# Sliding attention layer in woven steps, and the bias row store ahead of the first projection

## Chip, cores and metric

One Trainium2 chip, one core. The metric is the device time of one execution in microseconds, the lower the better. The kernel runs TensorE (matmuls; its weight loads are shown as PEld), VectorE (DVE), ScalarE (ACT), GpSimd (POOL) and the DMA engines; SyncE (SP) issues the weight DMAs, ScalarE's queue the others.

## What is computed

Two blocks in a row on 512 tokens of 1024 features, float32. The first block has two layers (a mixer, a convolutional feed-forward and a gated embedding each); the second block has one layer of two attentions and an expert layer. The change touches the second layer's mixer:

```python
def mixer_c(h, w_in, q_norm, k_norm, sinks, rel_bias, w_out):
    proj = h @ w_in
    q, k, v = jnp.split(proj, [SW_HEADS * SW_DIM, (SW_HEADS + SW_KV_HEADS) * SW_DIM], axis=-1)
    q = rmsnorm(q.reshape(B, S, SW_HEADS, SW_DIM), q_norm)
    k = rmsnorm(k.reshape(B, S, SW_KV_HEADS, SW_DIM), k_norm)
    ...
        logits = jnp.einsum('bqhgd,bkhd->bhgqk', qn, kn) * scale + bias
        logits = jnp.where(mn, logits, -jnp.inf)
        m = jnp.maximum(jnp.max(logits, axis=-1, keepdims=True), sink)
        e = jnp.exp(logits - m)
        w = e / (jnp.sum(e, axis=-1, keepdims=True) + jnp.exp(sink - m))
        return jnp.einsum('bhgqk,bkhd->bqhgd', w, vn)
    ...
    return o.reshape(B, S, C_OUT) @ w_out
```

There are 16 query heads and 4 key heads of 64 features; blocks of 128 queries see their own block of keys and the one before (the first block only its own). The bias is a table of distances (`window_rows`); a similar table (`chunk_rows`) serves the second block. Both tables are built at the start, from the inputs.

## The kernel before

Activations are kept by feature: a tile is 128 features by 512 tokens. Every weight product is made in three matmuls of 128x512 a k-step, from operands split into a high and a low part (`split_product`, L189). Weights come as one stream of slots of 16 tiles (1 MB). SyncE loads a slot into `weights_raw`; GpSimd splits it (L2608 makes the high part, L2610 the low part) into one of two places in `weights_split`; TensorE frees a place with the first matmul of the next slot (`release_previous`). So GpSimd splits a slot each time TensorE enters a new one.

`program` lists the stages; each engine runs its part of each stage in this order, and where a stage has `meet=True` all three engines wait for each other at its end. Layers other than the two touched here mostly do without meetings: they hand PSUM banks on one by one (`Bank`, `Held`), in an order that the program writes out.

`mixer_ab` (first layer's mixer): inputs are loaded by ScalarE's queue, `first_norm` norms them, `normed_heads` projects 20 tiles and the values (L189; VectorE evacuates at L1195, ScalarE the values at L594), and then the stage of `bias_rows` makes the bias rows: TensorE multiplies a small table (L1462), VectorE makes the chunk rows (L1468, L1470) and copies the window rows (L1473), ScalarE issues two DMAs that store them 128 times over (L1477, L1480). A meeting ends it. The stick-breaking attention (L879, L909) follows. In `normed_heads` the first tile goes ahead of the norm's sums; every evacuation needs `rstd`, which waits for ScalarE's square root (L481) and VectorE's reciprocal (L492). There are eight banks.

`mixer_c` (the sliding attention layer) has these stages, with a meeting after each but the last: `normed_heads` for 8 query and 2 key tiles and the values (L1509, L594); a norm stage for these ten tiles (squares L1547, sums L1521, root L1554, reciprocal L1530, product L1533) and eight copies of keys (L1560); `softmax_attention` in a loop of four rounds of 16 units (a head and a query block each: score L1266, bias L1319, maximum L1325, shift L1330, exponent L1420 and that of the sink L1423, transpose L1280, copy L1430, values L1290, scaling by the inverse L1377); `turn_split` (L822) back to features; `residual_product`, whose tiles are added to the residual (L621) and normed for the feed-forward (L444, L453, L460).

`branches` (the second block's attentions) is unchanged. It has steps of two scores (L1747), with dense k-steps between them (L189), the turn of the step before (L1764), and the value products of the step before that (L1785); on VectorE biased scores (L1886), small sums (L1893, L1895), joining (L1898); on ScalarE exponents (L2015).

## Time and profile before

| | us |
|---|---|
| median of 3 runs (lowest, highest) | 3805.36 (3803.27, 3808.34) |
| profiled execution, its own time | 3805.51 |
| its span from first to last instruction | 3803.7 |
| TensorE busy | 3556.4 (93%) |
| VectorE busy | 2068.8 (54%) |
| ScalarE busy | 922.9 (24%) |
| GpSimd busy | 1829.8 (48%) |

Shares are over the whole span; TensorE's ends are modelled, so 93% does not mean that it works at its peak. The chain that ended last is TensorE for 80% of the span and L189 alone for 71%. Mean granted clock of TensorE is 0.949 of full speed; of the 40 slices of the page it is 0.8, 0.8, 0.5, 0.5 in those from 856 to 1236 us.

### The profile page before, as it was taken

What the parts mean: (1) busy time and instruction counts of PE and PEld (TensorE: products, weight loads), DVE (VectorE), ACT (ScalarE), POOL (GpSimd) and SP (SyncE); (2) the same over time, 40 slices, a digit from 0 to 9 for tenths busy, and PEclk for the clock granted to TensorE, in tenths of its full rate; (3) what the DMA queues carried; (4) which work ended last, traced back from release to release, by engine and by line L of the source; (5) the groups of instructions that cost most, each with busy time, mean ns of one, the idle gap of its engine ahead of it and who ended that gap; (6) DMA issues with size and microseconds to landing.
All of it is one profiled execution on the core that took longest, in us unless ns stands there. A gap on an engine that the chain in (4) does not pass through costs nothing.

```text
span 3803.7 us, 44488 instructions
## 1 busy us (share of the span) xinstructions
PE 3556.4 (93%) x16442; PEld 2914.4 (77%) x16442; DVE 2068.8 (54%) x3513; ACT 922.9 (24%) x1682; POOL 1829.8 (48%) x548
## 2 busy tenths in 40 slices
PE   7865699998789999989999999999999999999999
PEld 6754588887556788878677878888888888888887
DVE  2125564426454645161662288885555437777776
ACT  1054322202144222020453121113333311111111
POOL 5500156654300556555333556665444456666664
PEclk9987799998855999999999999999999999999999
DMA  3250032222200222222111223434444475655552
GB/s 140 93 56 0 11 105 90 99 100 78 78 0 11 95 97 92 100 94 89 56 62 67 100 93 140 143 140 161 179 193 182 172 249 197 201 180 204 192 188 100
DMA packets 134077, 439.85 MB, mean 116 GB/s; under 512 B 7019, under 2 KB 76692, under 8 KB 97044
## 3 DMA queue, kind: packets, MB, share of 16 engines
q1 hardware_dynamic: 39168, 285.23, 21.3%
q10 hardware_dynamic: 94740, 152.22, 12.1%
q8 instruction: 124, 2.03, 0.2%
q14 instruction: 45, 0.37, 0.0%
HBM read 362.46 MB, written 74.96 MB: 115 GB/s over the span
## 4 chain that ended last, share of the span: by engine, by line
PE 80%; DVE 5%; ACT 2%; issue 1%; ACTq 0%; DVEq 0%; DMA 0%
PE banks L189 71%; PE banks L2218 3%; PE banks L1266 1%; DVE memory L460 1%; PE banks L1290 1%; DVE memory L1898 1%; DVE memory L1530 1%; PE banks L1280 1%; PE banks L1785 1%; ACT memory L2015 1%; PE banks L1747 1%; DVE memory L453 0%; PE banks L1764 0%; DVE memory L1895 0%; PE banks L468 0%
## 5 line engine op out<-in xcount | busy, mean ns | idle before, releaser
L189 PE MATMUL banks<-memory,weights_split 128*128 128x512 f32 x9456 | 2217.9, 394 | 57.9 <-DVE memory L453 31.5
L189 PEld LDWEIGHTS banks<-memory,weights_split 128*128 128x128 f32 x9456 | 1772.2, 189 | 448.7 <-DVE memory L453 35.2
L2608 POOL TENSOR_SCALAR weights_split<-weights_raw 128x2048 fp32r<-128x2048 f32 x272 | 543.5, 1998 | 1927.1 <-issue 1130.5
L2610 POOL TENSOR_TENSOR weights_split<-weights_raw,weights_split 128x2048 fp32r<-128x2048 f32 x272 | 1286.1, 4728 | 22.7
L189 PE MATMUL banks<-weights_split,memory 128*128 128x512 f32 (+1 forms) x3648 | 817.4, 386 | 0.0
L189 PEld LDWEIGHTS banks<-weights_split,memory 128*128 128x128 f32 x3648 | 678.3, 188 | 138.4
L2366 DVE TENSOR_TENSOR memory<-memory,memory 128x512 f32<-128x512 f32 x128 | 356.0, 2782 | 51.1 <-DMA memory<-hidden 44.5
L2351 DVE TENSOR_SCALAR memory<-banks,memory 128x128 f32<-128x128 f32 x512 | 174.4, 403 | 210.4 <-PE banks L2218 204.8
L2372 DVE TENSOR_TENSOR memory<-memory,memory 128x512 fp32r<-128x512 f32 x128 | 176.6, 1379 | 160.9 <-ACT memory L2486 160.9
L2486 ACT ACTIVATE memory<-memory 128x512 fp32r<-128x512 f32 x128 | 80.7, 632 | 601.1 <-PE banks L189 579.2
L2419 ACT ACTIVATE memory<-banks 128x512 f32<-128x512 f32 x128 | 76.5, 597 | 550.7 <-PE banks L189 550.7
L666 DVE TENSOR_TENSOR banks<-banks,memory 128x512 f32<-128x512 f32 x88 | 61.3, 699 | 231.8 <-PE banks L189 231.8
L621 DVE TENSOR_TENSOR residual<-banks,residual 128x512 f32<-128x512 f32 x32 | 22.1, 690 | 222.6 <-PE banks L189 222.6
L2431 ACT ACTIVATE memory<-banks 128x512 f32<-128x512 f32 x128 | 131.6, 1133 | 21.0 <-PE banks L2218 21.0
L714 ACT ACTIVATE memory<-banks,memory 128x512 f32<-128x512 f32 x88 | 68.6, 781 | 263.3 <-DVE banks L666 263.3
L2218 PEld LDWEIGHTS banks<-memory,memory 128*128 128x128 f32 x1024 | 124.1, 191 | 5.0
L2218 PE MATMUL banks<-memory,memory 128*128 128x128 f32 x1024 | 124.5, 275 | 0.0
L460 DVE TENSOR_TENSOR memory<-memory,memory 128x512 f32<-128x512 f32 x56 | 123.9, 2212 | 0.0
L444 ACT ACTIVATE memory<-residual,memory 128x512 fp32r<-128x512 f32 x64 | 46.2, 722 | 320.0 <-DVE residual L621 273.6
L453 DVE SCALAR_TENSOR_TENSOR memory<-residual,memory,memory 128x512 fp32r<-128x512 f32 x64 | 96.3, 1504 | 33.3 <-ACT memory L444 33.3
L1124 PE MATMUL banks<-memory,memory 128*128 128x128 f32 x256 | 47.5, 351 | 49.0 <-DVE memory L1049 47.4
L1266 PE MATMUL banks<-memory,memory 64*128 64x256 f32 (+1 forms) x128 | 66.8, 643 | 26.1 <-DVE memory L1579 26.1
(237 smaller groups left out, 2510.8 us busy)
## 6 DMA issues: line engine op xcount, KB each, us to landing
weights_raw<-in_weights SPq DMA_DIRECT2D x272, 1024.0 KB, 4.8
hidden<-memory ACTq DMA_DIRECT2D x64, 512.0 KB, 2.6
routing<-memory ACTq DMA_DIRECT2D x16, 2048.0 KB, 6.3
memory<-routing ACTq DMA_DIRECT2D x32, 1024.0 KB, 6.5
memory<-hidden ACTq DMA_DIRECT2D x32, 1024.0 KB, 8.9
window_rows<-memory ACTq DMA_DIRECT2D x1, 3064.0 KB
chunk_rows<-memory ACTq DMA_DIRECT2D x1, 2556.0 KB
residual<-in_x ACTq DMA_DIRECT2D x4, 512.0 KB, 11.3
```

The source lines that it names most:

```text
L189: last = k.nc.tensor.matmul(out, left[a], right[b], start=start and n == 0, stop=stop and n == 2, skip_group_check=True)
L453: v.scalar_tensor_tensor(out=self.out.low(n), in0=cut(k.h, n * 512, 512), scalar=k.column(self.gain, n), in1=self.out.high(n).bitcast(F32) ...
L460: v.tensor_tensor(self.total, self.squares[0] if n == 1 else self.total, self.squares[n % 2], ALU.add).then_inc(k.summed, 1)
L1266: k.nc.tensor.matmul(k.banks[:, u % 3, 0:blocks * P], query, key, start=True, stop=True).then_inc(scored, 1)
L2218: last = mm(score_banks[g % DEPTH].memory[:, s], rows[g % DEPTH][:, s], cols[g % DEPTH][:, s], start=True, stop=True, skip_group_check=True)
L2351: last = v.tensor_scalar(rows[g % DEPTH][:, t * P:(t + 1) * P], iota, cut(turned, at, 1), cut(turned, 2 * TOKENS + at, 1), ALU.is_equal, A ...
L2366: v.tensor_tensor(gated[e % 2].rearrange("p (c t) -> p c t", c=TOKENS // PORTION), cut(kept[place], e % GROUP * 512, 512).rearrange("p (c ...
L2372: v.tensor_tensor(operand.low(e % 4), gated[e % 2], operand.high(e % 4).bitcast(F32), ALU.subtract).then_inc(ready, 1)
L2431: a.activation(by_token[:, at:at + BATCH, :], score_banks[g % DEPTH].memory.rearrange("p (t n) -> p t n", t=BATCH), ACT.Copy).then_inc(mat ...
L2486: a.activation(operand.high(e % 4), gated[e % 2], ACT.Copy).then_inc(high_made, 1)
L2608: k.nc.gpsimd.tensor_scalar(high, raw, 1.0, 1.0, ALU.mult, ALU.mult).then_inc(k.high_made, 1)
L2610: k.nc.gpsimd.tensor_tensor(low, raw, high.bitcast(F32), ALU.subtract).then_inc(k.weights_ready[place], 1)
```

## The change

The kernel after has a function `window_layer` in place of `mixer_c` and `softmax_attention`. It works on pairs of heads (PAIRS = 8), four steps a pair, 32 steps. Ahead of the steps come four product tiles (two of keys, first two of queries), their norms and the values. Each step issues the scores of a pair for one query block, a k-step of a later weight product, the turn of the probabilities of the step before, sometimes the square sums of a later query tile, another k-step, and the value products of two steps before. The k-steps are those of the other six query tiles and then of the output product. The turn is a matmul with a diagonal matrix that holds the inverse of the totals, so that it transposes and divides at once; the value product gives its result by feature. Scores carry the opposite sign, and bias, smallest value and sink are taken in one VectorE instruction. The weight tiles are reordered to fit. In `mixer_ab` the stage of the bias rows goes ahead of the projection, has no meeting, and stores the window rows negated; the projection now ends with a meeting.

```diff
@@ -1197,9 +1197,10 @@
...
-    projected = normed_heads(k, first, 20, evacuate, 2, 512, lambda part, b: cut(values, b * 1024 + part * 512, 512))
     load_rows, rows_stage, await_rows = bias_rows(k)
-    stages = [Stage(scalar=load_all, meet=False), normed_first, projected, rows_stage]
+    projected = normed_heads(k, first, 20, evacuate, 2, 512, lambda part, b: cut(values, b * 1024 + part * 512, 512),
+                             meet=True)
+    stages = [Stage(scalar=load_all, meet=False), normed_first, rows_stage, projected]
     with k.scope(at=HN_AT):
...
-        v.tensor_copy(rows[0:SW_HEADS, :], bank.memory[0:SW_HEADS, 0:BUCKET_ROWS]).then_inc(k.freed["vector"], 1)
+        v.tensor_scalar(rows[0:SW_HEADS, :], bank.memory[0:SW_HEADS, 0:BUCKET_ROWS], -1.0, None,
+                        ALU.mult).then_inc(k.freed["vector"], 1)
...
-    return load, Stage(tensor, vector, scalar), await_written
+    return load, Stage(tensor, vector, scalar, meet=False), await_written
...
+    score_banks = [Held(k, 2 + f, (biased, 2 * STEPS - 1 + f)) for f in range(2)]
+    turn_banks = [Held(k, 4 + f, [free for w, free in enumerate(turn_free) if w % 2 == f][-1]) for f in range(2)]
+    out_banks = [Held(k, 6 + f, (k.x_low, mixed.made_before + PAIRS - 1 + f)) for f in range(2)]
...
+        def score(t):
+            i, n = t // 4, t % 4
+            if t == 0:
+                pe.wait_ge(keys_made, 2 * SW_KV // 2)
+                pe.wait_ge(keys_copied, SW_KV)
+            if n == 0:
+                pe.wait_ge(q_made, i + 1)
+            for f in range(2):
+                if t == 0:
+                    score_banks[f].await_free(pe)
+                else:
+                    pe.wait_ge(biased, 2 * (t - 1) + f + 1)
+                rows = slice(64 * f, 64 * f + 64)
+                mm(cut(score_banks[f].memory, 0, width(t)), normed_q[i % 2][rows, n * P:(n + 1) * P],
+                   cut(key_pairs[rows, :], i // 2 * 512 + (n + 1) * P - width(t), width(t)), start=True,
+                   stop=True).then_inc(scored, 1)
...
+        def turn_probs(t):
+            bank = await_turn_bank(turn_uses["probs", t])
+            pe.wait_ge(turning_made, 2 * t + 2)
+            for f in range(2):
+                for at in range(0, width(t), P):
+                    last = mm(cut(bank, f * 256 + at, P), cut(buffer(t, f), at, P), turn_matrix(t, f), start=True,
+                              stop=True)
+            last.then_inc(turned_up, 1)
...
+            pe.wait_ge(copied, t + 1)
+            bank = out_banks[i % 2].memory
+            for at in range(0, width(t), P):
+                block = n + 1 - (width(t) - at) // P
+                for f in range(2):
+                    last = mm(bank[64 * f:64 * f + 64, n * P:(n + 1) * P],
+                              cut(values, block * 256 + i // 2 * 64, 64), cut(turned[t % 3], f * 256 + at, P),
+                              start=at == 0, stop=at + P == width(t), skip_group_check=True)
...
+            for tiles, parts in (((0, 1, 2, 3), range(6)), ((0, 1, 2, 3), (6,)), ((0, 1, 2, 3), (7,)),
+                                 ((4, 5, 6, 7), range(8))):
...
+        opening_product(0)
+        normed.tensor_sums(pe)
+        opening_product(1)
+        opening_product(2)
+        opening_sums(0)
+        opening_sums(1)
+        opening_product(3)
+        opening_sums(2)
+        opening_values(0)
+        opening_sums(3)
+        for b in range(1, BLOCKS):
+            opening_values(b)
...
+        for t in range(STEPS + 2):
+            late = t >= STEPS
+            if t < STEPS:
+                score(t)
+            advance(2 if late else 1)
+            if 1 <= t <= STEPS:
+                turn_probs(t - 1)
+            if ("sums", (t + 3) // 4) in turn_uses and t % 4 == 1:
+                sum_squares((t + 3) // 4)
+            advance(4 if late else 1 if t < 24 or t % 4 in (0, 1, 3) and t != 29 and t != 31 else 0)
+            if t >= 2:
+                apply(t - 2)
+        for _ in work:
+            pass
...
+            v.tensor_tensor_reduce(out=buffer(t, f), in0=cut(score_banks[f].memory, 0, width(t)),
+                                   in1=cut(table, at, width(t)), scale=1.0,
+                                   scalar=cut(minus_sinks, 2 * i + f, 1), op0=ALU.add, op1=ALU.min,
+                                   accum_out=one(shift, t, f)).then_inc(biased, 1)
...
+        def shift_sinks(t):
+            dve.wait_ge(biased, 2 * t + 2)
+            v.tensor_tensor(pair(sink_shift, t), pair(shift, t), cut(minus_sinks, t // 4 * 2, 2),
+                            ALU.subtract).then_inc(sinks_shifted, 1)
+
+        def turn_matrices(t):
+            dve.wait_ge(sinks_exped, t + 1)
+            v.tensor_tensor(pair(total, t), pair(total, t), pair(sink_exp, t), ALU.add).then_inc(small_made, 1)
+            dve.wait_ge(small_made, 2 * t + 2)
+            v.reciprocal(pair(inverse, t), pair(total, t)).then_inc(small_made, 1)
+            dve.wait_ge(small_made, 2 * t + 3)
+            for f in range(2):
+                v.tensor_scalar(turn_matrix(t, f), k.const("ident"), one(inverse, t, f), None,
+                                ALU.mult).then_inc(turning_made, 1)
+
+        def invert_half(i, half):
+            dve.wait_ge(rooted, i - 1)
+            part = cut(deviation, half * 256, 256)
+            v.reciprocal(part, part).then_inc(inverted, 1)
+
+        def normalise(i):
+            dve.wait_ge(inverted, 4 + 2 * (i - 1))
+            v.scalar_tensor_tensor(out=normed_q[i % 2], in0=raw_q, scalar=k.column("q_norm"), in1=deviation,
+                                   op0=ALU.mult, op1=ALU.mult).then_inc(q_made, 1)
...
+        for n in range(4):
+            evacuate(made[n], first_raw[n], 1.0 if n < 2 else -(64 ** -0.5))
+        opening_keys(0)
+        opening_keys(1)
+        opening_queries(0)
+        opening_queries(1)
+        for t in range(LAST + 1):
+            i = t // 4
+            if t < STEPS:
+                for f in range(2):
+                    biased_scores(t, f)
+                shift_sinks(t)
+            if t % 4 == 0 and 2 <= i + 1 < PAIRS:
+                evacuate(dense[i - 1], raw_q, -(64 ** -0.5))
+            if t >= 6 and t % 4 == 2:
+                low(i - 1)
+            if t < STEPS:
+                turn_matrices(t)
+            if 2 <= i + 1 < PAIRS:
+                if t % 4 >= 2:
+                    invert_half(i + 1, t % 4 - 2)
+                if t % 4 == 3:
+                    normalise(i + 1)
+        for n in range(D_TILES + 1):
...
+        def exponent(t, f):
+            act.wait_ge(biased, 2 * t + f + 1)
+            a.activation(buffer(t, f), buffer(t, f), ACT.Exp, bias=one(shift, t, f), scale=-1.0,
+                         accum_out=one(total, t, f)).then_inc(exped, 1)
+
+        def sink_exponents(t):
+            act.wait_ge(sinks_shifted, t + 1)
+            act.wait_ge(exped, 2 * t + 2)
+            a.activation(pair(sink_exp, t), pair(sink_shift, t), ACT.Exp).then_inc(sinks_exped, 1)
...
+        for t in range(LAST + 1):
+            i = t // 4
+            if t >= 6 and t % 4 == 2:
+                high(i - 1)
+            if t < STEPS:
+                for f in range(2):
+                    exponent(t, f)
+                sink_exponents(t)
+            if 1 <= t <= STEPS:
+                copy(t - 1)
+            if t % 4 == 0 and 2 <= i + 1 < PAIRS:
+                square(i + 1)
+            if t % 4 == 1 and 2 <= i + 1 < PAIRS:
+                root(i + 1)
...
-            lambda: mixer_c(k, common, mix1_norm, ffn_norm[1]), lambda: layer(1),
+            lambda: window_layer(k, common, mix1_norm, ffn_norm[1]), lambda: layer(1),
...
-    tiles += [feature(c[:, 0:1280], 8), by_token(c[:, 1280:1536]), feature(a["c_w_out"][0], 8)] + layer_rest(1)
+    window_out = feature(a["c_w_out"][0], 8).reshape(8, 8, P, P)
+    tiles += [feature(c[:, 1024:1280], 8), feature(c[:, 0:256], 8), by_token(c[:, 1280:1536]), feature(c[:, 256:1024], 8)]
+    tiles += [window_out[:4, 0:6].reshape(-1, P, P), window_out[:4, 6], window_out[:4, 7], window_out[4:].reshape(-1, P, P)]
+    tiles += layer_rest(1)
```

## Rows read from the trace of the kernel before

**Rows 1.** Busy us by stretch: PE, PEld, DVE, ACT, POOL; clock, DMA share, GB/s.
```profile
180.00:200.00 20.00, 0.64 (x2) 0.00 (x0) 0.65 (x2) 0.83 (x2) 0.00 (x0) 0.63 0.47 58
...
936.60:1005.00 68.40, 67.71 (x325) 57.13 (x325) 10.82 (x13) 3.79 (x7) 32.62 (x10) 0.93 0.24 81
...
1005.00:1055.40 50.40, 15.68 (x20) 4.07 (x20) 41.26 (x22) 17.07 (x28) 0.00 (x0) 0.59 0.13 42
...
1055.40:1215.10 159.70, 143.60 (x464) 101.09 (x464) 84.73 (x390) 69.16 (x260) 0.00 (x0) 0.50 0.00 0
...
1860.00:1960.00 100.00, 95.78 (x498) 71.08 (x496) 80.09 (x181) 53.38 (x130) 34.29 (x11) 1.00 0.15 53
```

**Rows 2.** Timeline of the sliding attention layer: start us, us, engine, line, operation.
```profile
936.57 1.65 PE L189 MATMUL banks<-memory,weights_split 128*128 128x512 f32 x3 [5.98 <-DVE memory L453]
...
949.32 0.69 DVE L1509 TENSOR_TENSOR memory<-banks,memory 128x512 f32<-128x512 f32 x1 [4.56 <-PE banks L189]
...
992.64 11.67 PE L189 MATMUL banks<-weights_split,memory 128*128 128x256 f32 x96
...
1266.64 0.69 DVE L621 TENSOR_TENSOR residual<-banks,residual 128x512 f32<-128x512 f32 x1 [1.10 <-PE banks L189]
...
1275.15 9.03 PE L189 MATMUL banks<-memory,weights_split 128*128 128x512 f32 x27 [3.79 <-DVE memory L453]
```

**Rows 3.** Timeline of TensorE in the steps of `branches`.
```profile
1853.62 0.64 PEld L1785 LDWEIGHTS banks<-memory,memory 128*128 128x128 f32 x4
...
1854.38 0.30 PEld L1747 LDWEIGHTS banks<-memory,memory 64*128 64x128 f32 x4
...
1854.80 1.23 PEld L189 LDWEIGHTS banks<-memory,weights_split 128*128 128x128 f32 x6
...
1859.32 0.70 PE L1747 MATMUL banks<-memory,memory 64*128 64x256 f32 x4
...
1859.95 1.24 PEld L189 LDWEIGHTS banks<-memory,weights_split 128*128 128x128 f32 x6 [0.33 <-issue]
...
1863.65 1.09 PEld L1785 LDWEIGHTS banks<-memory,memory 128*128 128x128 f32 x8
...
1864.86 0.30 PEld L1747 LDWEIGHTS banks<-memory,memory 64*128 64x128 f32 x4
```

**Rows 4.** Timeline, VectorE and ScalarE operations that overlap no split by GpSimd.
```profile
317.46 0.48 DVE L984 TENSOR_SCALAR memory<-memory,memory 128x512 f32<-128x512 f32 x1
...
1020.23 3.35 DVE L1530 RECIPROCAL memory<-memory 128x512 f32<-128x512 f32 x1
...
1853.77 0.75 DVE L1898 SCALAR_TENSOR_TENSOR memory<-memory,memory,memory 128x512 f32<-128x512 f32 x1
...
1862.78 0.41 DVE L1886 CUSTOM_DVE_ANT_0 memory<-banks,memory 128x256 f32<-128x256 f32 x1
...
1863.23 0.51 ACT L2015 ACTIVATE memory<-memory,memory 128x256 f32<-128x256 f32 x1 [5.12 <-DVE memory L1886]
...
1864.36 0.16 DVE L1893 RECIPROCAL memory<-memory 128x1 f32<-128x1 f32 x1 [0.81 <-ACT memory L2015]
```

**Rows 5.** Timeline, VectorE beside GpSimd's second operation of a split.
```profile
138.85 4.70 DVE L1470 TENSOR_SCALAR memory<-memory 8x256 f32<-8x256 f32 x1
...
1857.44 4.76 DVE L1898 SCALAR_TENSOR_TENSOR memory<-memory,memory,memory 128x128 f32<-128x128 f32 x1
1857.49 4.56 POOL L2610 TENSOR_TENSOR weights_split<-weights_raw,weights_split 128x2048 fp32r<-128x2048 f32 x1
```

**Rows 6.** Timeline of the first layer's start and of the bias rows.
```profile
29.10 0.68 DVE L460 TENSOR_TENSOR memory<-memory,memory 128x512 f32<-128x512 f32 x1
...
60.26 0.69 DVE L1195 SCALAR_TENSOR_TENSOR memory<-banks,memory 128x512 f32<-128x512 f32 x1 [4.75 <-PE banks L189]
...
181.26 17.87 ACTq L1480 DMA_DIRECT2D window_rows<-memory  x1
...
199.90 0.43 DVE L909 COPY memory<-memory 128x512 f32 x1 [18.67 <-ACTq L2576]
```

515 lines of the change are left out of this document (239 added, 276 removed).

## Prediction

> **What bounds the kernel now.** I read the windows first. In the fourth layer part, the sliding attention, TensorE works at its upper clock level while the dense products run, then stands almost idle for 50.4 us (15.7 busy), then spends 159.7 us in the attention at a granted clock of 0.50, the lower of the two levels (1.2 GHz), with VectorE at 84.7 us, ScalarE at 69.2 and GpSimd, which splits the weights, at nothing; TensorE's 143.6 are stretched by the clock and by ends that are only modelled [rows 1]. So this stretch is bound less by one engine than by a chain that passes from one to the next, and the weight stream stands still meanwhile. The last window of [rows 1] is the other attention of this kernel, `branches`, which already puts dense products between its steps: clock 1.00, TensorE 95.8 of 100 us busy. It is the best model of the new layer, and most of my prices come from it. Second, the timeline of the layer's landmarks: it begins with three products at 936.57, and the feed-forward after it can go on at 1275.15 [rows 2]. That is 338.6 us, of which the dense work is small: a tile of eight k-steps takes 0.69 + 4.75 = 5.44 us [rows 6], so a k-step ("partial", three matmuls) takes 0.68 us, and a value block 11.67 / 4 = 2.9 us [rows 2]. 10 and 8 tiles and 4 value blocks are 98 + 12 = 110 us. Third, the timeline around 180 us for the bias rows: the last ACT issue takes 17.87 us, and the next stage waits for it [rows 6].
>
> **Part one, the opening.** Removed: the norm stage and the three meetings around it. New: TensorE makes two key tiles, two query tiles, four square sums and the values, and VectorE norms only these four tiles. TensorE: the second tile is ready at 949.3 as before, then two tiles to 954.8 and about 961.7 with two sums of 0.75 us between, then sum, value, sum and three values: 974.9. (A square sum is one f32 product of 512 columns in two passes: 2 x 0.227 from the tile time, and 0.2 to 0.4 of fill as at the changes in [rows 3].) VectorE is later. From 962.6 it has four reciprocals of 3.35 us [rows 4] and six operations from SBUF of 0.75 [rows 4]. GpSimd's second operation of a split locks such operations out for its whole length: an operation on 128 columns shows 4.76 us, where the same on 512 columns takes 0.75 when GpSimd rests [rows 4], and a tensor_scalar of eight rows shows 4.70 [rows 5]. Splits start with each slot of 16 partials (962.9, about 980.5 here) and last 6.6 us (32.6 for ten instructions [rows 1]; the second 4.6 [rows 5], so the first about 2). So: reciprocal to 966.0, key writes held until 969.5 and done at 970.9; second keys 975.7; first queries 979.8. The first score then goes at 980.0, 5.1 us after TensorE ran dry. Its first partial starts the next split, the second queries' reciprocal ends at 983.3, and its last write is held until 987.9. Only then come the biased scores of step 0, and step 1 starts at 988.7. TensorE is cold there (lower level, as in every gap of [rows 1]); with this, steps 1 to 3 take 5, 4.5 and 4.4 us (no value products at first): step 4 starts at 1002.4.
>
> **Part two, one group of four steps.** Prices on TensorE, from start to start of the weight loads [rows 3]: scores of a pair of heads, 0.42 with one key block and 0.63 with two; products of 128x128 f32, 0.76 for four instructions, 1.21 for eight. A step with two key blocks has eight in the turn and eight in the value products, its first step of a group four. The value products have a form that the trace does not show, 64 stationary columns: between 0.6 (two heads side by side) and 1.2 us; I take 1.2, the row nearest to it. Per step score + partial + turn of the step before + partial + values of two steps before: 4.18, 4.70 (with a square sum), 3.95, 4.39 = 17.2 us.
>
> VectorE per step: it begins 0.75 after the score's start [rows 3], a biased score takes 0.41, the pair 0.8, and ScalarE's two exponents begin 0.45 after the first and last 1.1 to 1.2 [rows 4], the sinks' exponent 0.3. Then total, reciprocal and two tiny matrices: the 128x128 tensor_scalar is not in the trace, between 0.15 and 0.55 (its 512-column form [rows 4]); I take 0.2, since a quarter of the columns is nearer to the low end. The turn may start 2.9 us after VectorE began (2.5 with one block). In the third step half a reciprocal (1.7) follows, in the fourth 1.7 + 0.75 for the normed queries of the next pair. Evacuating a query tile and making the low part lie in the wait for the exponents and cost nothing; without that wait they would cost 1.4 us a group.
>
> With a group's first score at 0, scores start at 0, 4.2, 8.9, 12.8; VectorE begins the third step at 9.6 and leaves it at 14.2, begins the fourth only then and has the next queries at 19.8. The next group starts at **19.9**, not 17.2: the waits move from ScalarE's chain to the query norm. At steps 8, 16 and 24 a split begins as well. The turn matrices of that step, due at 3.1, wait for the split's end at 7.25 and are ready at 8.1; the next starts are 11.5 and 15.5, the group takes **22.6**. Groups 1, 3, 5 take 19.9, groups 2, 4, 6 take 22.6, the last one, without norms and with fewer partials, 14.4: 1002.4 + 59.7 + 67.8 + 14.4 = 1144.3.
>
> **Part three, the tail.** Steps 32 and 33 hold twelve partials and the last turn and values, 11.8 us; 112 - 72 = 40 partials remain, 27.2 us; the last product's residual row at 1266.64 to 1275.15 [rows 2] becomes the same 8.7 us with the same lock. The next layer goes on at 1144.3 + 11.8 + 27.2 + 8.7 = 1192.0. **Gain 83.2 us.** The reordered weight tiles are as many as before and cost nothing: GpSimd needs 6.6 us for a slot that TensorE never eats in under 10.9. Table loads of ScalarE's square root fall into its idle time.
>
> **Part four, bias rows.** The row product, two rows on VectorE and two DMA issues go ahead of the projection. Behind it, only the meeting remains: VectorE's 199.90 becomes about 181.3 (ScalarE had done its value copies when it came to the issue at 181.26), **18.6 us** [rows 6]. In front, TensorE's 0.8 us falls into waits that it has anyway. ScalarE however has the 17.87 us issue before the square root on which all banks' release waits: VectorE's norm is done at 29.8, the rows and the first issue at 32, the second until 50, root and reciprocal until 56, first bank free at 57. TensorE has five further free banks and needs the sixth at 60.2, where [rows 6] has the fifth one emptied. Slack 3 us. If weights (DMA share 0.24 in the dense stretch [rows 1]) stretch the issue by as much, it is 2 us late. Between 0 and 5 us of loss I take 1: 17.6 us gain.
>
> **Sum.** The profiled execution took 3805.5 us (span 3803.7 and 1.8 around it), 0.1 over the median. 3805.5 - 83.2 - 17.6 = 3704.7, say **3704**.
>
> **Rivals.**
> A, *shorter groups*. If the value products of the two heads run side by side (0.6), a plain group takes 18.8 and a locked one 22.0, the other stretches 5 less: 3693. With VectorE's chain alone as bound (2.5 + 2.95 + 4.65 + 5.6 and links, 16.5 a group) it would be 3684. The Trainium skill, "TensorE: Matmul & The Clock Gate", section on packing small matmuls, says that matmuls with outputs in distinct column groups run concurrently; that is this rival, and no row of the trace before shows the form. Chance 0.16.
> B, *locks twice*. The split may catch the matrices of step 8j and again the queries' write or the tiny subtraction for the sinks, since it starts when TensorE reaches the slot, not at a fixed place. One more lock of 4.6 us in each of four slots: 3722. Chance 0.15.
> C, *the row stage gains nothing*: the issue takes long under the weight loads and the projection stops for all of it. For it: the DMA share is 0.47 behind the old place with almost no weights moving [rows 1]. Against it: five free banks. 3722. Chance 0.08.
> D, *the turn is dear*. Before, the turn was a transpose against the identity; now it is a true f32 product. If its passes were twice as dear as the value products of `branches` (0.22 us more for each of 14 blocks a group, 3.1 us, of which 1.3 reach the end of a plain group), the layer is 9 to 12 us longer: 3714. The Trainium skill, the same page, table of terms, has a transpose mode that is 4 times faster for FP32, which speaks against this fold; [rows 3] show 1.21 us for eight true f32 instructions. Chance 0.04.
> E, *the clock stays at its lower level*. The old attention had 0.50, the gap before step 1 is there, and each locked group has a wait of 2.6 us. In the steps alone that would give about +85: 3790, chance 0.03. The slower side: it stays from the first wait through the tail. 112 partials cost 0.68 more each (76), and the small products, 94 us at the upper level, 70 more, less some 32 of waits that they fill: +115, **3820**. It decides from 102 us of loss on. Against it: `branches` has waits of the same kind at 1.00 [rows 1]. Chance 0.02.
> F, the change does not take effect in the order written (nothing moves): 3805, chance 0.01.
>
> **How the numbers follow.** The forecast has 0.51. Its own doubt is about 10 us. The range must hold the forecast, A to D, so from A's lower end to B and C with that doubt: 3674 to 3738. Measurement tells 0.2% (7.6 us) from no change; faster by more: all but E's second case, F and part of E's first, 0.95; within: 0.02; slower: 0.03.
>
> **What would show it.** Window 980 to 1145 at clock about 1.00 with TensorE over 85% busy; first score near 980 and a gap behind it; starts of the scores of steps 8, 12, 16, 20 19 to 23 us apart, with the longer ones where a split begins; VectorE's tensor_scalar of a locked step at 4 us or more; ScalarE's square root of the first norm near 51 to 56 us; VectorE's first copy of the stick-breaking stage near 181. If groups take under 17 or over 25 us, or the clock falls below 0.9 in the steps, the sum is wrong.

## The result, and the profile after

The kernel after takes 3720.24 us (median of 4 runs, 3718.21 to 3722.16), the kernel before beside it 3804.51 (3803.27 to 3808.34): ratio 0.978, 95% interval 0.976 to 0.979. The forecast was 3704 with a range from 3674 to 3738. The direction, the size and the layer that pays were right; the gain came out 84 us, not 101. The profiled execution took 3722.16, its span is 3720.3 (before 3803.7), mean granted clock 0.970 (before 0.949). TensorE's busy time fell from 3556.4 to 3494.7 us only: the rest of the gain is idle time that is gone.

Page of the kernel after, parts 1 and 2: busy time, and the granted clock in 40 slices of 93 us.
```profile
span 3720.3 us, 43665 instructions
...
PE 3494.7 (94%) x16522; PEld 2867.9 (77%) x16522; DVE 2058.2 (55%) x3418; ACT 921.5 (25%) x1623; POOL 1829.0 (49%) x548
...
PEclk9987799999889999999999999999999999999999
```
The two slices at 0.5 are gone; those of the new layer stand at 0.8 and 0.8.

Timeline of the kernel after, the same landmarks as [rows 2, 6].
```profile
191.78 0.43 DVE L909 COPY memory<-memory 128x512 f32 x1 [43.89 <-ACTq L2689]
...
930.76 1.65 PE L189 MATMUL banks<-memory,weights_split 128*128 128x512 f32 x3 [5.97 <-DVE memory L453]
...
1151.34 32.30 PE L189 MATMUL banks<-memory,weights_split 128*128 128x512 f32 x141
...
1187.42 8.95 PE L189 MATMUL banks<-memory,weights_split 128*128 128x512 f32 x27 [3.79 <-DVE memory L453]
```
The difference of the spans, 83.4 us, taken apart by them:

| stretch | before | after | gain | predicted |
|---|---|---|---|---|
| to VectorE's first copy of stick-breaking (L909) | 199.90 | 191.78 | 8.1 | 17.6 |
| stick-breaking, L909 to L970 | 111.4 | 113.8 | -2.5 | 0 |
| from there to the sliding layer | 625.3 | 625.1 | 0.2 | 0 |
| sliding layer | 338.58 | 256.66 | 81.9 | 83.2 |
| everything behind it | 2528.6 | 2532.9 | -4.3 | 0 |

So the sliding layer met its forecast within 1.3 us, and the shortfall of 17 us lies in the bias rows (9.5), in stick-breaking and behind the layer.

Windows of the kernel after in the new layer: the opening, then groups of four steps (cut at the first score of each); the last row is the last group with the two late steps. Columns as in [rows 1].
```profile
930.76:974.60 43.84, 38.59 (x189) 31.61 (x190) 24.37 (x17) 12.46 (x20) 13.03 (x4) 0.89 0.25 89
974.60:994.70 20.10, 15.54 (x74) 10.43 (x74) 14.91 (x38) 6.21 (x23) 6.74 (x2) 0.75 0.24 83
994.70:1014.00 19.30, 15.06 (x102) 10.26 (x100) 12.31 (x41) 11.07 (x29) 0.00 (x0) 0.95 0.01 2
1014.00:1037.50 23.50, 17.54 (x100) 11.97 (x100) 17.41 (x41) 11.07 (x29) 6.44 (x2) 0.86 0.13 45
1037.50:1059.20 21.70, 17.45 (x98) 12.06 (x99) 12.29 (x41) 11.07 (x29) 0.00 (x0) 0.88 0.00 1
...
1127.10:1151.30 24.20, 24.17 (x147) 18.32 (x147) 7.62 (x37) 7.89 (x26) 6.20 (x2) 0.93 0.00 1
```
A group with a split on GpSimd (6.44 us in the POOL column) takes 23.2 to 23.5 us, one without 21.5 and 21.7, the first without 19.3. TensorE is busy for 15.1 to 17.5 us of a group, at a granted clock of 0.86 to 0.95. What it waits for, by the view of waits for 974 to 1151 us, TensorE (us in total, times, longest):
```profile
PE banks L1422 <- DVE memory L1590: 25.5, 6, 4.3
PE banks L1438 <- DVE memory L1580: 10.0, 7, 3.5
PE banks L1422 <- DVE memory L1547: 5.3, 1, 5.3
```
The first line is the score of a new pair behind VectorE's product of the next queries, at the end of every group with a norm. The second is the turn behind its diagonal matrices. The timeline shows both, at the end of a group and in the locked step behind it:
```profile
1011.39 1.74 DVE L1586 RECIPROCAL memory<-memory 128x256 f32<-128x256 f32 x1
1013.17 0.75 DVE L1590 SCALAR_TENSOR_TENSOR memory<-memory,memory,memory 128x512 f32<-128x512 f32 x1
...
1013.98 0.80 PE L1422 MATMUL banks<-memory,memory 64*128 64x128 f32 x4 [4.24 <-DVE memory L1590]
...
1014.70 1.65 PE L189 MATMUL banks<-memory,weights_split 128*128 128x512 f32 x3
...
1017.66 4.54 POOL L2723 TENSOR_TENSOR weights_split<-weights_raw,weights_split 128x2048 fp32r<-128x2048 f32 x1
...
1017.82 4.67 DVE L1580 TENSOR_SCALAR memory<-memory,memory 128x128 f32<-128x128 f32 x2
...
1020.32 0.97 PE L189 MATMUL banks<-memory,weights_split 128*128 128x512 f32 x3
...
1022.64 0.68 PE L1438 MATMUL banks<-memory,memory 128*128 128x128 f32 x4 [1.35 <-DVE memory L1580]
```
Two things are to be seen. The second half of the reciprocal and the product stand behind everything else of the fourth step. And the same three matmuls take 1.65 us right behind the wait and 0.97 six us later: the granted clock falls to its lower level with the gap, so a wait is paid for twice.

The opening of the kernel after, weights of the first projection (for POOL, what its idle time ended with):
```profile
30.80 18.45 ACTq L1269 DMA_DIRECT2D window_rows<-memory  x1
...
50.57 0.69 ACT L481 ACTIVATE memory<-banks,memory 128x512 f32<-128x512 f32 x1
...
66.67 1.91 POOL L2721 TENSOR_SCALAR weights_split<-weights_raw 128x2048 fp32r<-128x2048 f32 x1 [10.12 <-DMA weights_raw<-in_weights]
...
73.38 23.62 PE L189 MATMUL banks<-memory,weights_split 128*128 128x512 f32 x96 [2.09 <-POOL weights_split L2723]
99.61 23.66 PE L189 MATMUL banks<-memory,weights_split 128*128 128x512 f32 x96 [2.61 <-POOL weights_split L2723]
125.12 22.05 PE L189 MATMUL banks<-memory,weights_split 128*128 128x512 f32 x96 [1.85 <-POOL weights_split L2723]
147.00 43.68 PE L189 MATMUL banks<-weights_split,memory 128*128 128x512 f32 x192
```
Three times GpSimd waits 10 to 12 us for a slot that has not landed, and TensorE about 2 us behind it. Behind the first two of these waits TensorE falls to the lower clock (0.67 and 0.66 in the 5 us that follow; 23.6 us for 96 matmuls where the last line has 43.68 / 2 = 21.8). Behind the third it does not (1.00, and 22.05 us). In the kernel before, the value products that start here at 147.00 start at 136.22.

### The profile page after: what moved, and what is told of

Same layout as the page of the kernel before. It is cut to its first block, busy times and chain, and to the rows that moved or that the text cites. A ratio compares the mean times of both kernels' runs of the same rounds, so it can differ in the third digit from the quotient of the medians.

```text
span 3720.3 us, 43665 instructions
## 1 busy us (share of the span) xinstructions
PE 3494.7 (94%) x16522; PEld 2867.9 (77%) x16522; DVE 2058.2 (55%) x3418; ACT 921.5 (25%) x1623; POOL 1829.0 (49%) x548
## 3 DMA queue, kind: packets, MB, share of 16 engines
q1 hardware_dynamic: 39168, 285.23, 21.5%
## 4 chain that ended last, share of the span: by engine, by line
PE 78%; DVE 6%; ACT 3%; issue 1%; DMA 0%; ACTq 0%; DVEq 0%
PE banks L189 71%; PE banks L2331 3%; DVE memory L460 1%; DVE memory L2011 1%; PE banks L1898 1%; ACT memory L2128 1%; PE banks L1860 1%; DVE memory L1586 1%; ACT memory L1662 1%; PE banks L1438 0%; DVE memory L453 0%; DVE memory L1532 0%; PE banks L1877 0%; DVE memory L2008 0%; PE banks L468 0%
## 5 line engine op out<-in xcount | busy, mean ns | idle before, releaser
L189 PE MATMUL banks<-memory,weights_split 128*128 128x512 f32 x9456 | 2249.8, 396 | 44.2 <-DVE memory L453 30.8
L2467 DVE TENSOR_TENSOR memory<-banks,memory 128x512 f32<-128x512 f32 x128 | 87.2, 681 | 0.0
```

The costliest lines, as they stand in the source:

```text
L189: last = k.nc.tensor.matmul(out, left[a], right[b], start=start and n == 0, stop=stop and n == 2, skip_group_check=True)
L2467: v.tensor_tensor(cols[g % DEPTH].rearrange("p (t n) -> p t n", t=BATCH), iota.unsqueeze(1).broadcast_to(three), cut(turned, TOKENS + g * ...
```

## Experiments

**The bias rows: where did 9.5 us go?** Theory 1: the two stores (2556 and 3064 KB by the page's list of DMA issues) share the DMA engines with the weights, and the weights come late. Rival: the move brings what was predicted, and the shortfall is elsewhere. Two kernels move this stage alone, one in each direction.

```diff
-    stages = [Stage(scalar=load_all, meet=False), normed_first, rows_stage, projected]
+    stages = [Stage(scalar=load_all, meet=False), normed_first, projected, rows_stage]
```


> The kernel after with the bias rows stage put back behind the first projection (and the meeting of the engines put back). Theory 1, late weights: in the kernel after the two stores of bias rows share the DMA engines with the projection's weights, so the move gains only the 8.1 us by which VectorE's first copy of the stick stage comes earlier (191.78 against 199.90); this run is 3720.2 + 8 = about 3728 us. Rival, the prediction's own term: the move is worth 17.6 us and the shortfall is elsewhere; this run is 3720.2 + 17.6 = about 3738 us.

Measured: 3724.6 us (ratio to before 0.979, interval 0.978 to 0.980). So the change of the sliding layer alone is worth 80.2 us beside its kernel before (3804.8).

The same edit the other way round, in the kernel before (with the meeting moved along):

> The kernel before with the bias rows stage moved ahead of the first projection, and nothing else. Theory 1, late weights: 3804.5 - 8 = about 3796 us. Rival, the prediction's own term: 3804.5 - 17.6 = about 3787 us. If the two parts of the change help or hinder each other, this run and the one that undoes the move will not show the same difference.

Measured: 3798.9 us (ratio 0.998, interval 0.997 to 0.999). The two runs give 4.4 and 5.9 us for the move: even less than theory 1 said, and far from 17.6. The executions of the second spread widely, from 3791 to 3807 us, and the profiled one is the longest of them. In it TensorE waits 9.6 us in three waits for late weights, one of 5.1 us:
```profile
73.41 22.05 PE L189 MATMUL banks<-memory,weights_split 128*128 128x512 f32 x96 [2.14 <-POOL weights_split L2611]
100.56 23.58 PE L189 MATMUL banks<-memory,weights_split 128*128 128x512 f32 x96 [5.11 <-POOL weights_split L2611]
126.52 23.62 PE L189 MATMUL banks<-memory,weights_split 128*128 128x512 f32 x96 [2.38 <-POOL weights_split L2611]
```
The run with the old order has none of these waits and starts its value products at 135.09. The list of DMA issues from 28 to 130 us has the weight loads with their median time to landing, first in the kernel after, then in the kernel before:
```profile
weights_raw<-in_weights SPq DMA_DIRECT2D x8, 1024.0 KB, 16.1
```
```profile
weights_raw<-in_weights SPq DMA_DIRECT2D x8, 1024.0 KB, 4.8
```

Now the cause by itself: the larger store is issued behind the projection, all else stays.
```diff
         act.dma_start(k.dram["chunk_rows"], chunk_rows[0:CH_HEADS, :].unsqueeze(1).broadcast_to(
             [CH_HEADS, P, TOKENS + P - 1])).then_inc(written, 16)
+    def store_window(act):
         bank.await_read(act)
         act.dma_start(k.dram["window_rows"], rows[0:SW_HEADS, :].unsqueeze(1).broadcast_to(
             [SW_HEADS, P, BUCKET_ROWS])).then_inc(written, 16)
...
+    def values_then_store(act):
+        evacuate_values(act)
+        store_window(act)
```


> The kernel after, with the larger store (window_rows, 17.9 us of issue on ScalarE) issued behind ScalarE's part of the first projection, not ahead of it. Theory 1, late weights: the weights arrive on time, the projection ends up to 10 us earlier, and ScalarE issues the store while the next stage's first loads are awaited; 3720.2 - 10 = about 3710 us, or down to nothing gained if ScalarE's issue now holds up the stick stage's first steps. Rival, the store is not what makes the weights late (other loads do): 3720 us.

Measured: 3709.9 us (ratio 0.975, interval 0.973 to 0.976), 10.4 us under the kernel after. Timeline of this run:
```profile
30.30 0.82 ACTq L1273 DMA_DIRECT2D chunk_rows<-memory  x1
...
72.12 67.44 PE L189 MATMUL banks<-memory,weights_split 128*128 128x512 f32 x288 [2.08 <-POOL weights_split L2731]
139.40 43.68 PE L189 MATMUL banks<-weights_split,memory 128*128 128x512 f32 x192
...
183.12 0.63 ACTq L1277 DMA_DIRECT2D window_rows<-memory  x1
...
184.52 0.43 DVE L909 COPY memory<-memory 128x512 f32 x1 [44.23 <-ACTq L2697]
```
One of TensorE's three waits is left; GpSimd still waits for two late slots (10.1 and 9.6 us). Not all of the 10.4 us belongs to the edit: of the 9.9 us between the two profiles 7.3 stand at VectorE's first copy (184.52 against 191.78), and 2.8 behind the sliding layer, where the program is the same. And the issue that takes 17.87 us in the kernel before [rows 6], 18.45 in the kernel after and 20.53 in the run before this one takes 0.63 here, with the same bytes: it was long wherever it stood right behind the other store. The rival of the prediction that blames ScalarE's issue (C) falls too: in the kernel after the issue is over at 49.3 and the root runs at 50.57, and TensorE has no wait for a bank in the whole projection. That the stores' traffic makes the weights late, and not their issue, is inferred: with the large store gone from this place the other's issue takes 0.82 us, and slots are late all the same. A kernel that stores 8 of the 128 copies at the old place, which would have parted the two, gave no time.

**The groups: what sets 21.7 us?** Theory 2: VectorE's own order. It begins the fourth step only after its work of the third, and the next queries come at the end of the fourth. First, take the twelve half reciprocals away:
```diff
-                if t % 4 >= 2:
-                    invert_half(i + 1, t % 4 - 2)
...
         def normalise(i):
-            dve.wait_ge(inverted, 4 + 2 * (i - 1))
+            dve.wait_ge(rooted, i - 1)
```


> The kernel after without the twelve half reciprocals of the query norm in the window steps; the queries of head pairs 2 to 7 are multiplied by their root instead of its inverse, so the scores of those pairs differ from the reference. Theory 2, VectorE's own order ends each group: a group of four steps is as long as VectorE's work in it, TensorE waits 4.25 us for the product at its end six times, and without 2 x 1.75 us the wait shrinks to about 0.8: 3720.2 - 6 x 3.5 = about 3699 us. Rival, the prediction's own working (TensorE's instructions and the lock set the group, VectorE's reciprocals are beside them): about 3720 us.

Measured: 3693.3 us (ratio 0.971, interval 0.969 to 0.972), 27 us less, not 21; from the first score to the end of the layer it is 24.0 us (188.8 against 212.8). The wait on L1590 falls from 25.5 us to 4.6 in all. TensorE's instructions and the lock alone do not set the group.

Then the same work, only earlier:
```diff
-            if t < STEPS:
-                turn_matrices(t)
             if 2 <= i + 1 < PAIRS:
                 if t % 4 >= 2:
                     invert_half(i + 1, t % 4 - 2)
                 if t % 4 == 3:
                     normalise(i + 1)
+            if t < STEPS:
+                turn_matrices(t)
```


> The kernel after with VectorE's half reciprocals and the query product issued ahead of the turn matrices of their step, not behind; nothing is left out. Theory 2, VectorE's order ends the group: the first half then lies in the 2.0 us in which VectorE waits for ScalarE's sink exponents (L1575 behind L1668), and the product is ready about 1.7 us earlier in its own step, so the 4.25 us wait of TensorE shrinks to about 1: 3720.2 - 6 x 3.3 = about 3700 us, less what TensorE or the later turn matrices give back. Rival (as for the run without reciprocals): 3720 us, or slower, since the turn matrices come 2.5 us later and the turn waits for them.

Measured: 3693.3 us (ratio 0.971, interval 0.969 to 0.972): the same time without leaving anything out, since the reciprocals now lie where VectorE waited for ScalarE (27.6 us in 32 waits on the sinks' exponent in the kernel after, 11.2 in 17 here). Windows of this run, by group:
```profile
990.01:1006.04 16.03, 15.09 (x101) 10.28 (x99) 11.59 (x38) 11.08 (x29) 0.00 (x0) 1.00 0.01 2
1006.04:1027.08 21.04, 16.67 (x99) 11.09 (x99) 17.37 (x42) 11.10 (x29) 6.43 (x2) 0.92 0.16 51
1027.08:1043.09 16.01, 15.07 (x98) 10.28 (x98) 12.14 (x42) 11.08 (x29) 0.00 (x0) 1.00 0.00 1
```
A group without a split takes 16.0 us, 15.1 of them TensorE's, at clock 1.00. It was 21.7: 3.3 us of wait are gone, as expected, and some 2 us more, because TensorE no longer falls to the lower clock behind the wait. From the first score to the end of the layer the edit is worth 212.8 - 190.3 = 22.5 us, nearly as much as leaving the reciprocals out. So of what both runs gained beyond their forecasts about 3 us (24.0 against 21, 22.5 against 20) come from the steps, and about as much is not their doing: the opening of this run took 40.6 us, not 43.8, by the clock alone, and that of the run before it 40.7. Windows of the first 10 us of the layer, first the kernel after, then this run:
```profile
930.76:935.76 5.00, 5.00 (x14) 3.68 (x15) 1.43 (x2) 1.77 (x3) 0.00 (x0) 0.50 0.46 170
935.76:940.76 5.00, 5.00 (x13) 3.88 (x13) 3.37 (x4) 0.79 (x2) 0.00 (x0) 0.54 0.00 0
```
```profile
929.37:934.37 5.00, 5.00 (x18) 3.66 (x19) 1.63 (x2) 1.93 (x3) 0.00 (x0) 0.72 0.49 179
934.37:939.37 5.00, 5.00 (x23) 4.13 (x22) 3.62 (x5) 0.63 (x1) 0.00 (x0) 1.00 0.00 0
```
The instructions are the same, both follow a wait of 6.0 us, and one has 27 matmuls in its first 10 us, the other 41.

**Does it matter that the products are spread over the steps?** All eight k-steps of a group go into its first step.
```diff
-            advance(2 if late else 1)
+            advance(2 if late else 1 if t >= 24 else 8 if t % 4 == 0 else 0)
...
-            advance(4 if late else 1 if t < 24
+            advance(4 if late else 0 if t < 24 else 1 if t < 24
```


> The kernel after with the 8 partial products of a dense projection placed together in the first step of each of the first six groups, and none in the other three steps; nothing is left out. Theory 2, VectorE's and ScalarE's loop sets the steps: it still takes some 4 us a step without them, the bunch of 7.6 us fills the first step, and the group stays at 21 to 23 us: 3720 us, within 8. Rival, the products are what hides the waits inside each step (the reason for placing them one by one): steps 1 to 3 become as long as before but without 1.9 us of useful work each, which the first step then pays: 6 x 3 x 1.9 = 34 us more, 3754 us.

Measured: 3731.7 us (ratio 0.981, interval 0.980 to 0.983), 11.5 us more than the kernel after: between the two theories, nearer to the first, but outside the 8 us that it allowed. From the first score to the end the layer is 13.6 us longer (226.4 against 212.8). TensorE now waits 24.6 us in 15 waits for the turn matrices (10.0 in 7 before), so the k-steps do cover that wait; the wait for the next queries stays (22.4 us in six). The fine spread is worth 12 to 14 us of the 82; the rest comes from doing the products beside the steps at all, or from other parts of the rewrite, which no run here takes apart.

**Both edits.**

> The kernel after with both edits: the larger store of bias rows issued behind the first projection (measured alone: 3709.9, 10.4 us less) and the query norm ahead of the turn matrices. If the two lie in different layers and do not touch, the gains add: by theory 2, 3720.2 - 10.4 - 20 = about 3690 us; by its rival 3710 us.

Measured: 3688.9 us (ratio 0.969, interval 0.968 to 0.970). It is faster than with either edit alone, but the late store adds 4.4 us here, not 10.4. In the profile VectorE's first copy comes 5.7 us earlier than without it (184.79 against 190.44), and the opening of the layer gives 3.3 back: 43.9 us at clock 0.50 and 0.54, as in the kernel after.

**The lock.** In the run with the early norm a group with a split takes 5.2 us more than one without. Its timeline:
```profile
1007.14 1.90 POOL L2721 TENSOR_SCALAR weights_split<-weights_raw 128x2048 fp32r<-128x2048 f32 x1 [28.55 <-issue]
...
1007.34 1.71 DVE L1570 TENSOR_TENSOR memory<-memory 128x2 f32<-128x2 f32 x1
...
1009.13 4.53 POOL L2723 TENSOR_TENSOR weights_split<-weights_raw,weights_split 128x2048 fp32r<-128x2048 f32 x1
...
1009.58 4.10 DVE L1575 TENSOR_TENSOR memory<-memory 128x2 f32<-128x2 f32 x1
...
1014.54 1.19 PE L1438 MATMUL banks<-memory,memory 128*128 128x128 f32 x4 [3.42 <-DVE memory L1580]
```
Two numbers a partition, 1.71 and 4.10 us. Theory 3: only such operations of VectorE (two inputs, or a tensor_scalar, all in SBUF) are held, so they should leave VectorE in these steps.
```diff
+    def on_scalar(t):
+        return t % 8 < 2
...
+                    a.activation(one(sink_exp, t, f), one(shift, t, f), ACT.Exp,
+                                 bias=k.column("sinks", t // 4 * 2 + f)).then_inc(exped, 1)
...
+                    a.activation(one(total, t, f), one(total, t, f), ACT.Identity,
+                                 bias=one(sink_exp, t, f)).then_inc(sinks_exped, 1)
...
+                a.activation(turn_matrix(t, f), k.const("ident"), ACT.Copy,
+                             scale=one(inverse, t, f)).then_inc(turning_made, 1)
```


> The kernel with both edits (3688.9 us) in which, in the steps 0, 1, 8, 9, 16, 17, 24 and 25, the two sums of the sinks and totals and the two turn matrices are made on ScalarE, and VectorE does only the reciprocal between them; nothing is left out. In the kernel with the early query norm a group with a weight split on GpSimd lasts 21.0 to 21.3 us and one without 16.0, and the 5.2 us between them stand on VectorE's tiny sums of 128x2 (1.71 and 4.10 us, where they take 0.16 elsewhere) beside GpSimd's L2721 and L2723. Theory 3, the lock: those instructions are the ones that wait for GpSimd; on ScalarE they do not, and three groups lose 3 to 4.5 us each and the first some 3: 3688.9 - 12 to 16 = about 3675 us. Rival, GpSimd holds up whatever VectorE does beside it (the reciprocal, the biased scores), or the work on ScalarE lengthens the steps as much: 3689 us, within 3.

Measured: 3676.3 us (ratio 0.966, interval 0.965 to 0.968), 12.6 us less. The locked groups take 17.4 to 18.0 us (21.1 and 21.3 before), the first four steps 18.8 (20.0 before), a gain of 1.2 there and not 3. Timeline:
```profile
1000.92 4.56 POOL L2765 TENSOR_TENSOR weights_split<-weights_raw,weights_split 128x2048 fp32r<-128x2048 f32 x1
...
1002.05 0.48 DVE L1583 CUSTOM_DVE_ANT_0 memory<-banks,memory,memory 128x256 f32<-128x256 f32 x1 [1.02 <-PE banks L1442]
...
1004.82 0.17 DVE L1598 RECIPROCAL memory<-memory 128x2 f32<-128x2 f32 x1 [1.88 <-ACT memory L1698]
```
Beside the same GpSimd operation the biased score (one input in PSUM) and the reciprocal keep their usual 0.48 and 0.17 us. The lock theory holds, and its rival falls. The Trainium skill, "SBUF — State Buffer", section on the two separate sides, has a port pair that the two engines take for a whole instruction, VectorE only in a two-port mode or with two inputs from SBUF; the trace agrees. With only the first of the two steps (`t % 8 == 0`):

> As the run before it, but only in the steps 0, 8, 16 and 24. Theory 3: GpSimd is still in its 4.5 us when the next step's 128x2 sum comes, which is then held for the rest of it, some 2 to 3 us; so about half of the gain is left, 3681 us. Rival: 3689 us, as with both steps.

Measured: 3676.0 us (ratio 0.966, interval 0.965 to 0.967). The lock moves to the next step as expected, 2.54 us of it:
```profile
1004.93 4.58 POOL L2765 TENSOR_TENSOR weights_split<-weights_raw,weights_split 128x2048 fp32r<-128x2048 f32 x1
...
1006.98 2.54 DVE L1592 TENSOR_TENSOR memory<-memory 128x2 f32<-128x2 f32 x1
```
but it costs less than it shows: first score to end of layer is 180.4 us, against 178.2 with both steps and 190.4 with neither. Four fifths of the gain, not half, and in the medians no difference at all. I had counted the lock's length as the loss; it seems that some of it lies under k-steps that TensorE has anyway. The work on ScalarE has a price too: with both steps there, VectorE's reciprocal in the second waits 1.88 us for ScalarE (the line at 1004.82). Which of the two it is, no run takes apart.

## Why the prediction was right, and where it was not

**What bounds the kernel** held: a chain between engines at the lower clock, with the weight stream at rest; the model `branches` [rows 1, 3, 4] gave usable prices.

**Part one.** The first score was put 43.4 us behind the layer's start, with TensorE dry for 5.1; measured 43.9 and 5.3. Step 4 was put at 65.8, measured 63.9. Right, though part of the size is luck: 3 us of it hang on the clock. And the lock fell elsewhere: the last write of queries, put as held for 4.6 us, took 1.19 us (at 977.66), and the tiny subtraction for the sinks behind it 3.82 (at 979.43).

**Part two.** The mechanism was the one named, "the waits move from ScalarE's chain to the query norm", and six waits of 4.25 us show it. The sizes: plain groups 19.3, 21.7 and 21.5 where 19.9 stood, locked ones 23.5, 23.2 and 23.3 where 22.6 stood, 5.0 us more in all. Two terms were mis-sized. The clock: I priced every instruction at the upper level; a score shows 0.49 us there and three matmuls of a k-step 0.97, and behind each wait they show 0.80 and 1.65; `branches` with its mean of 1.00 [rows 1] had misled me. And ScalarE's table loads, said to fall into idle time: behind the root the exponents' load of 1.28 us comes first, and VectorE waits 1.98 us for the sinks' exponent at 1029.80, in the third step, where the group before has 1.60 in its third and 0.85 is usual in others. The price of the value products was wrong the other way: eight take 0.66 us, rival A's price, not 1.2. The Trainium skill, "TensorE: Matmul & The Clock Gate", section on packing small matmuls, has outputs in distinct column groups run at the same time; the trace agrees. It did not matter in the kernel after, where TensorE was not the bound, so rival A's time of 3693 failed while its price was true. It matters once VectorE's order is mended: the run with the early norm reaches 16.0 us a group, below even the 16.5 that rival A gave VectorE's chain, and takes 3693.3.

Rival B, a second lock, is there in the record but not in its price: the 128x2 sums are held as well as the matrices (L1575 1.18 us ahead of L1580's 4.67). A lock cost 1.8 us a group in the kernel after and 5.2 in the faster one: the shorter the chain, the less covers it. The prediction's own signs spoke against it here. It said that the sum is wrong if the clock falls below 0.9 in the steps, and expected about 1.00 with TensorE over 85% busy from 980 to 1145 us; the trace has 0.89 and 78% (129.5 of 165 us). The sum for the layer came out all the same, because the slower groups were made up for elsewhere. And the measured 3720 lies at the 3722 that rivals B and C gave, without either having happened as priced: no bank held up the projection, and the layer took 1.3 us more than put, not 18. D: eight instructions of the turn take 1.05 us busy, about what was put; the Trainium skill's transpose mode (same page, table of terms) was not tried. E: the steps have 0.75 to 0.95, not 0.5; F falls.

**Part three.** The last group and the two late steps took 24.2 us where 14.4 + 11.8 = 26.2 stood, the end 36.1 where 35.9 stood. The lock behind the last product fell where it was put: from the last residual row to the next layer it is 8.5 us (1178.91 to 1187.42), as before (1266.64 to 1275.15), with VectorE held beside GpSimd's split:
```profile
1178.91 0.69 DVE L1628 TENSOR_TENSOR residual<-banks,residual 128x512 f32<-128x512 f32 x1 [1.01 <-PE banks L189]
...
1181.68 5.03 DVE L460 TENSOR_TENSOR memory<-memory,memory 128x512 f32<-128x512 f32 x1
```
So the sum for the layer was out by 1.3 us only because errors of 2 to 5 us stand on both sides: the opening and the last group with the late steps 2 us less each, the six groups 5 us more.

**Part four** was the failure. The step is "If weights (DMA share 0.24 in the dense stretch) stretch the issue by as much, it is 2 us late": it asked what the weights do to the stores' issue and never what the stores do to the weights. The row that said so was there: a DMA share of 0.47 in the stretch behind the old place with almost no weights moving [rows 1]. The Trainium skill, "DMA: Bandwidth & Descriptors", section on issuing engines that are not separate DMA queues, says that transfers of all of them run on the same 16 DMA engines and interleave; the late slots agree with it. Theory 1 is right in kind (late slots, and 10.4 us back without the larger store, 7.3 of them in this stage). Its size, 8.1 us, was read from one profile; by the same mark the runs with the stage moved alone give 7.0 and 5.1 us, and 4.4 and 5.9 in the medians, with 6.5 us of waits in one profile and 9.6 in another.

**What the sum had no term for**: stick-breaking 2.5 us longer, and 4.3 behind the layer. Neither belongs to the change. Stick-breaking, the same program in all kernels, takes 111.4 us in the profile of before and between 109.5 and 114.3 in the others; the 114.3 is of the kernel with the old order of the bias rows. Everything behind the sliding layer takes 2528.6 us in one profile of before and 2532.6 in the profile with only the bias rows moved, which is the same program there; all profiles lie at 2528.6 to 2530.2 or at 2532.6 to 2533.3. What picks the one or the other is open.

## What to carry to other kernels

When a chain runs over several engines, look at the order within one engine first: work for the next round belongs in front of the wait for another engine, not behind it, which was worth nearly as much here as leaving the work out (22.5 against 24.0 us). Price a wait of TensorE with the slower matmuls behind it: most waits of 2 to 5 us here cost some 2 us on top, though two of about 2 us cost only 0.2. Before a store is moved beside a weight stream, count its bytes against that stream, and not only the time of its issue.

## What the runs showed of the hardware

A DMA issue on ScalarE's queue of 3064 KB took 17.9, 18.5 and 20.5 us right behind one of 2556 KB, and 0.63 us when 150 us lay between them. Weight loads of 1024 KB beside these two stores took 16.1 us to landing in the median, 4.8 without them. GpSimd's two operations of a weight split hold VectorE's tensor_scalar and two-input operations from SBUF for as long as they last, down to two columns (0.16 us became 1.71 and 4.10); a reciprocal of two columns (0.17) and a custom operation with one input in PSUM (0.48) are not held. TensorE after a wait of 6.0 us took 27 matmuls in 10 us in one profile and 41 in another, with the same instructions, and waits of 2.09 and 2.61 us in a dense stretch were followed by a granted clock of 0.67 and 0.66 over 5 us, which made the next 96 matmuls 1.8 us longer; behind waits of 1.85 and, in another profile, 2.14 us the clock was 1.00, and they took 0.2 us longer.
